# Differential attention: where VectorE combines a step's two maps, between or behind the next step's two maxima

## What is computed

```python
s = jnp.einsum('bqhmd,bkhmd->bhmqk', qi, k).astype(f32)
mask = key_chunk[None, :] <= qc[:, None]
s = jnp.where(mask, s, -jnp.inf)
p = jax.nn.softmax(s, axis=-1)
attn = p[:, :, 0] - lam * p[:, :, 1]
return jnp.einsum('bhqk,bkhe->bqhe', attn, v)
...
o = rms_norm(o, g_out) * (1.0 - lam_init)
return o.reshape(B, S, DIFF_WIDTH) * jax.nn.silu(z.astype(f32))
```

## Time and profile before

| | |
|---|---|
| median of 3 runs | 2306.05 us (2305.64 to 2307.0) |
| profiled execution | 2306.29 us, span 2304.4 us |
| TensorE busy | 2244.7 us, 97% of the span |
| VectorE busy | 1428.5 us, 62% |
| ScalarE busy | 1098.0 us, 48% |
| GpSimd busy | 653.2 us, 28% |

### The profile page before, as it was taken

How to read it: one execution, slowest core, us unless ns; L and a number is a source line. 1 busy time by engine, 2 the same in 40 slices (tenths; PEclk the granted TensorE clock), 3 DMA queues, 4 the chain that set the end, 5 groups by cost and what they waited for, 6 DMA issues and landing times. The chain is left out here.

```text
span 2304.4 us, 33214 instructions
## 1 busy us (share of the span) xinstructions
PE 2244.7 (97%) x12532; PEld 1852.2 (80%) x12532; DVE 1428.5 (62%) x1973; ACT 1098.0 (48%) x2343; POOL 653.2 (28%) x460
## 2 busy tenths in 40 slices
PE   6999999899999999989999999999999999999998
PEld 4887788778887778877888887787888888888887
DVE  5955524884553541586553266770688878787857
ACT  5445334773634523476443446663743333334743
POOL 2200020242310003043232123122315454547852
PEclk9999999999999999999999999999999999999999
DMA  7442260104112243002311100003223232336864
GB/s 264 142 133 83 87 223 2 38 1 165 74 46 75 74 161 113 19 20 82 111 64 49 60 1 1 21 19 138 92 69 113 94 120 87 125 105 226 280 198 163
DMA packets 160772, 226.70 MB, mean 98 GB/s; under 512 B 10685, under 2 KB 104292, under 8 KB 159078
## 3 DMA queue, kind: packets, MB, share of 16 engines
q1 hardware_dynamic: 159357, 224.51, 28.6%
q10 hardware_dynamic: 1256, 0.07, 0.0%
HBM read 176.05 MB, written 48.50 MB: 97 GB/s over the span
## 5 line engine op out<-in xcount | busy, mean ns | idle before, releaser
L4341 POOL TENSOR_TENSOR w_lo<-ffn_sums,w_hi 128x512 fp32r<-128x512 f32 x76 | 96.8, 1295 | 182.9 <-DVE hT_raw L4735 122.5
L814 POOL TENSOR_TENSOR w_lo<-difp_raw,w_hi 128x2048 fp32r<-128x2048 f32 x8 | 36.9, 4607 | 384.9 <-ACT w_hi L778 384.9
L889 PE MATMUL ps<-w_hi,hT_hi 128*128 128x512 f32 (+1 forms) x368 | 138.0, 385 | 2.9 <-PEq L4918 1.0
L889 PE MATMUL ps<-hT_hi,w_hi 128*128 128x512 f32 x360 | 140.5, 390 | 0.0
L889 PE MATMUL ps<-hT_lo,w_hi 128*128 128x512 f32 x360 | 140.1, 389 | 0.0
L889 PE MATMUL ps<-w_hi,hT_lo 128*128 128x512 f32 (+1 forms) x368 | 136.0, 370 | 0.0
L889 PE MATMUL ps<-w_lo,hT_hi 128*128 128x512 f32 (+1 forms) x336 | 129.4, 387 | 0.0
L889 PE MATMUL ps<-hT_hi,w_lo 128*128 128x512 f32 x328 | 127.7, 389 | 0.0
L4400 PE MATMUL ps<-ffn_t_hi,w_hi 128*128 128x512 f32 x304 | 118.4, 389 | 0.3 <-DVE ffn_u L4722 0.3
L4400 PE MATMUL ps<-ffn_t_hi,w_lo 128*128 128x512 f32 x304 | 118.3, 389 | 0.0
L4400 PE MATMUL ps<-ffn_t_lo,w_hi 128*128 128x512 f32 x304 | 118.3, 389 | 0.0
(11 more groups left out here) (638 smaller groups left out, 6615.0 us busy)
## 6 DMA issues: line engine op xcount, KB each, us to landing
ffn_raw<-in_ffn_w_up SPq DMA_DIRECT2D x40, 512.0 KB, 4.5
mix_gla<-in_w_ada SPq DMA_DIRECT2D x32, 512.0 KB, 3.5
xres<-big SPq DMA_DIRECT2D x24, 512.0 KB, 2.6
parts<-in_ffn_w_down SPq DMA_DIRECT2D x22, 512.0 KB, 5.8
wsum<-parts SPq DMA_DIRECT2D x11, 1024.0 KB, 7.7
ffn_sums<-hsum SPq DMA_DIRECT2D x44, 256.0 KB, 4.5
ffn_raw<-wsum SPq DMA_DIRECT2D x44, 256.0 KB, 4.4
glap_raw<-in_w_in SPq DMA_DIRECT2D x10, 1024.0 KB, 5.6
```

The source lines that it names most:

```text
L814: pool.tensor_tensor(m.w_lo[:, b, 0:w], raw[:, 0:w], m.w_hi[:, b, 0:w].bitcast(F32), ALU.subtract).then_inc(s_lo, 1)
L889: mm = nc.tensor.matmul(out[:, 0:r.shape[1]], l, r, start=(job.part != 1 and c == 0 and k == 0), stop=(job.evac and c == job.chunks - 1 an ...
L4341: pool.tensor_tensor(lo, op.source(n), hi.bitcast(F32), ALU.subtract).then_inc(s_lo, 1)
```

## The change

VectorE's queue in an iteration was: maximum of map 0, maximum of map 1 (both of step n + 1), combination of step n. It becomes: maximum of map 0, combination, maximum of map 1. All waits, buffers, instructions and the other engines' queues stay.

```diff
             for n in range(n_steps + 2):
                 if 1 < n + 1 < n_steps:
-                    for mp in range(2):
-                        start.maxima(dve, n + 1, mp)
+                    start.maxima(dve, n + 1, 0)
                 if 0 < n < n_steps:
                     start.combine(dve, n)
+                if 1 < n + 1 < n_steps:
+                    start.maxima(dve, n + 1, 1)
                 if n == n_steps + 1:
                     for i in ends(n, SUM_LAG):
                         sums(i)
```

## The result

The changed kernel takes 2327.08 us (4 runs, 2326.3 to 2331.25), the kernel before 2306.31 us beside it: 1.0091 times as long, 95% interval 1.0079 to 1.0103. That is 20.8 us slower where 10.9 were forecast: slower, as forecast, but outside the stated range, which ended at 2321.5 us.

A forecast was written before the change was run, and what follows sets the result against it. No engine is full; a ring of TensorE, ScalarE and VectorE bounds the stretches. The middle of 9.3 us (unstretched) and 12.5 us (present stretching), 10.9 us, on 2306.29 makes 2317.2, as a median 2317.0; range 2307.5 to 2321.5 us.

The forecast's parts named there:

- The ring: One step's loop through TensorE, ScalarE and VectorE: scores, transposes, emptying, exponentials, next scores; no engine is full.
- m1: VectorE's maximum of a step's map 1; forecast to end a whole combination later.
- h0: ScalarE's emptying of half 0 of the transposes' bank; it gates the next transposes.
- the stretches: The two spans, one per layer, where this code works; 92.7 and 92.0 us, forecast to become 98 us each.
- The earlier combination is worth 0: VectorE's combination starts 0.8 to 1.2 us earlier; booked as no gain, with 4.4 us as the far end.
- S - d' - I: Loss per step: e1's delay S, less the previous step's loss d', less ScalarE's idle time I; unstretched, 9.3 us.
- How long C takes in its new place: VectorE beside GpSimd: 9.3 us loss unstretched, 12.5 stretched as at present; the middle, 10.9 us, was taken.
- C: VectorE's combination of the step before; 1.46 us in the ordinary step 8, 2.83 in step 14.
- The upper bound: Four steps with weight conversions per layer each wait one more GpSimd instruction of 1.04 us: 20.8 us in all.
- m0: VectorE's maximum of a step's map 0; forecast to start no earlier in the new order.
- Rival (c), the clock: TensorE's new gaps of about 1 us lower its clock, up to 1.5 us per fall: 2320 to 2327; chance 0.10.
- e1: ScalarE's exponentials of map 1; forecast to start on m1's end, about 0.5 to 1.5 us later after its scores.

The follow-up runs named there:

- c4: Changed kernel with GpSimd's stage work cut to two columns and map 1's exponentials freed from the true maximum (constant bias, constant tile reduced): 2303.2 us.
- a1: Kernel before, old VectorE order, with GpSimd's tensor work in the attention stage cut to two columns per instruction: 2303.0 us.
- a2: Changed kernel, new VectorE order, with GpSimd's tensor work in the attention stage cut to two columns per instruction: 2311.3 us.
- c3: Kernel before, old VectorE order, with map 1's exponentials waiting for the combination and GpSimd's work in this stage made small: 2312.1 us.
- b1: Kernel before, old VectorE order, full GpSimd work; only ScalarE's exponentials of map 1 wait for the combination: 2325.0 us.
- a4: Kernel before with the new order only in the ten steps per layer that the sum booked as paying: 2321.6 us, ratio 1.0065.
- c1: Changed kernel with only GpSimd's low parts of the held weights cut to two columns: 2322.8 us, ratio 1.0070.
- c2: Changed kernel with only GpSimd's square, gating and norm of a finished tile cut to two columns: 2323.7 us, ratio 1.0072.
- b2: Changed kernel, full GpSimd work, with map 1's exponentials freed from the true maximum (constant bias, constant SBUF data reduced): 2313.3 us.

## Why the prediction was right and wrong, step by step

- *The ring and where it is paid*: right. ScalarE waits for m1 in nearly every step, TensorE's waits for the combination are gone, and those for h0 grew (1.4 us to 6.0 in layer 0). The waits ahead of scores stayed at 2.3 us, though they were forecast to grow, and the stretches are 103 and 104 us long where 98 were forecast.
- *The earlier combination is worth 0*: right. c4 against a1 is 0.2 us, with 4.4 us of waits at stake. VectorE does the same work up to `finish` in either order, so its next m0 starts no earlier.
- *S - d' - I, unstretched*: right in sum, 9.3 us against 8.3 (a2 less a1) and 9.0 (c3 less a1), in part by luck, since its parts are less good. In layer 1 of a2 against a1 step 4 costs 0.6 (0.98), step 14 0.7 (0.13), step 16 1.0 (0), step 17 nothing (1.0), and steps 7, 11 and 20 0.5 each, which I had at 0: the idle time behind the emptying of a turned output is not free. Errors of both signs that cancelled.
- *How long C takes in its new place*: this is the step that failed. I took the middle between unstretched and stretched as before, 1.6 us over both layers for GpSimd. It measured 20.8 - 8.3 = 12.5 us, with what it brings with it: the stretch of all combinations grew from 8.1 to 22.7 us. The upper bound named for this term, 20.8 us in all, is what came, for a reason near the one given (more GpSimd instructions met). That the figures agree is luck: the bound added 8.3 us of stretch to the present sum, while the stretch grew by 14.6 us, not all of it at a price, and the clock has a share. The growth was also spread over steps 4, 6, 10 and 15 to 19 and not only over those with weight conversions. And my range, 15.5 us above the median before, stopped short of that bound, which had been worked out from rows.
- *What I could have read*: GpSimd's square and gating in front of a combination, 2.3 us from the start of m0 on, under two maxima of 1.6 to 2.4 us. I left GpSimd's phase open and took a middle. For this work it is tied to VectorE: the square waits for `finish` and `sums`, so it starts with m0. The two maxima are the long operations of VectorE's step that GpSimd doesn't stretch (1022 ns before, 1023 after, 1026 in a2; the short `finish` of 128 columns keeps its time too, 283 ns before and 285 in a1), and the change took one of them from where GpSimd works. The low parts of the weights are tied to ScalarE instead, as b1 shows. The Trainium skill (SBUF — State Buffer, "SBUF: two separate sides") has both halves, the lock for two SBUF inputs and none for tensor_reduce, and the traces agree; the prediction named it and drew from it that C would be stretched as today, which holds only for an unchanged phase.
- *Rival (c), the clock*: it came, as a smaller part. The granted clock of the stretches fell from 0.96 and 0.98 to 0.95 and 0.95. Each layer of the changed kernel has one fall in mid-stretch, behind 1.88 us of idle time where the prediction named gaps of about 1 us; it costs at most 1.7 us, so both together at most 3.4 of the 20.8 us. a4 prices one. Both of its layers have the same idle time ahead of the same transposes, and only layer 1's is followed by a fall, as two rows of TensorE and windows over what follows show:

```profile
479.95 0.52 PE L2136 MATMUL ps<-ident,big 128*128 128x128 f32 x3 [1.88 <-ACT mix_diff L2304]
1047.93 0.52 PE L2136 MATMUL ps<-ident,big 128*128 128x128 f32 x3 [1.88 <-ACT mix_diff L2304]
```

```profile
480.00:484.00 4.00, 3.79 (x32) 3.33 (x34) 3.53 (x5) 2.57 (x5) 1.28 (x2) 1.00 0.00 0
1048.80:1052.20 3.40, 3.40 (x18) 3.28 (x17) 2.83 (x4) 2.59 (x5) 0.46 (x1) 0.50 0.00 0
```

From h0 of step 14 to h0 of step 21, layer 1 lost 4.2 us against the kernel before and layer 0 lost 2.8. By these 1.4 us, an estimate, the two falls of the changed kernel are 2.8 us, and they belong to its 12.5, since neither a1 nor a2 has one in mid-stretch. The profiled execution of the changed kernel also loses 1.2 us more in the first steps of layer 1 than in those of layer 0, and it took 4.2 us more than the median, so a part of its 25 us is not of the change.

What stays open: how the 12.5 us divide among GpSimd's instructions (c1 and c2 don't add up), and why a late e1 lets 14.7 us of stretch cost 12.9 us (b1 less c3) while an early combination with e1 on time lets 17.6 us cost 10.1 (b2 less c4). At 1.4 us each, the three falls of the clock in b1 account for 4.2 of the 12.9, and b2 has none; what is left, 8.7 against 10.1, doesn't differ beyond the noise. No run holds the clock, so its share is an estimate.

## What to carry to other kernels

Before an instruction is moved ahead of another in a queue, ask for whom the other one was a release, and count for that engine the time behind it until it is next needed; a next consumer that needs a bank cleared first has no air at all. Then lay the third engine's instructions beside the queue: if VectorE and GpSimd share a step, operations with two SBUF inputs should stand where GpSimd is idle and reductions where it works, and a move that changes this can cost more than the move itself (12.5 us against 8.3 here). And when a bound is worked out from rows, the range has to reach it.

## What the runs showed of the hardware

- A small factor of one column (L2059, 220 ns) takes up to 1305 ns in the changed kernel beside a GpSimd operation that reads SBUF, and the multiply-adds beside one between 0.7 and 1.1 us more than alone. The reductions keep their time: the maxima take 1022, 1023 and 1026 ns in three kernels, and those of b2, which read SBUF and not PSUM, 1044 ns with GpSimd's full work and 1045 ns with the small one (c4).
- The stretching is mutual: GpSimd was busy for 32.5 us in each stretch before and for 35.3 and 35.2 us after, with the same 28 instructions.
- In the changed kernel TensorE was idle for 1.88 us and then granted 0.50 for 3.4 us while always busy, once per layer. The same idle time of 1.88 us in layer 0 of a4 was followed by no fall, and against the kernel before that layer lost 1.4 us less from there on than layer 1 of a4, where one came.
